# Row norms of a three-layer transformer kernel: column sums and turned scales against matmul means, logarithm and exponential

## The chip, the cores and the metric

One core of one Trainium2 chip runs the whole program. The metric is the device time in microseconds (us), the median over runs.

## The reference, cut to what matters

Three layers are computed on 512 tokens of width 1024. Layer 1 is latent attention with an MLP, layer 2 is window attention with an MLP, and the third (a block of its own) has a wide input projection, attention over compressed, selected and windowed keys, a merge, and a gated feed-forward part. Each stage begins with a norm over the 1024 features of a token:

```python
def rmsnorm(x, g):
    xf = x.astype(jnp.float32)
    y = xf * lax.rsqrt(jnp.mean(xf * xf, axis=-1, keepdims=True) + EPS)
    return (y * g.astype(jnp.float32)).astype(x.dtype)
```

The third layer also normalises its keys and queries over the 64 features of each head (`rmsnorm_2(..., k_norm_g)`, `q_norm_g`), before `rope_2` rotates them.

## The kernel before, in words

Activations lie feature-major: partitions are 128 features, the free axis is the 512 tokens. Weights come as 301 tiles of 128x1024 float32 in the order of use. For each tile ScalarE copies `RAW` to a high part `WH` in fp32r (line 1129), GpSimd subtracts to get a low part `WL` (line 630), and TensorE does three fp32r products for each 128x128 block (`product`, lines 722 to 724): high by high, low by high, high by low. `dense` runs over the outputs of a stage; one output of 8 blocks is 24 matmuls of 512 columns. Outputs go round four PSUM banks (`RING`), so output o+4 waits until VectorE or ScalarE has drained output o. ScalarE keeps three tiles ahead (`AHEAD`): its step for output o can begin when TensorE has finished the tile of output o-1.

A norm's scale is not applied to the input: the raw products are multiplied by it when they are drained. So the scale is needed by the first drain of the stage, some outputs after its start. Before the change it is made thus: ScalarE squares, VectorE adds the squares over the 8 feature blocks (`add_square`, into `ACC` or `TMP`); TensorE sums over partitions into a column for each block of 128 tokens (`sums`, line 765: four fp32 matmuls whose moving operand has one column, each two records in the trace); VectorE adds EPS, ScalarE takes the root (`std`, line 1169), VectorE the reciprocal (`scale_columns`); TensorE turns the broadcast column into a row on all partitions (`scales`, line 778: four fp32 transposes of 128x128); VectorE copies that row to `RBC` (`scale_rows`). The token-major column itself (`RCOL`) is used where values are made token-major.

The head norms of the third layer are the same in small. R32 holds 6 tiles of two heads each. For tile j ScalarE squares, `head_sum(j)` (line 1009) sums per head into columns, three tiles at a time go through `head_var`, `head_std`, `head_scale`, then ScalarE widens the column of scales (`head_widen`, line 1431), and `head_spread(j)` (line 1018) turns it by four transposes. `head_norm`, `head_rotate`, `head_rotated` and `head_split` follow.

The place of each such step in stage `in2` is written by hand: `PE_AFTER`, `ACT_AFTER` and `DVE_AFTER` say after which output an engine does what. Every engine is in order. Other steps there are `compress`: step 1 after output 9 (32 fp32 matmuls), step 2 after output 12, which waits for ScalarE's Silu (`cmp_silu`, in ScalarE's step 11, line 1461), and step 3. Stage `in2` ends with `cmp_scores`, a softmax over compressed keys and the first weight tile of the gates.

Of the kernel before, what the change touches and what calls it, by code (L numbers as in the profile page):

```python
# [32 lines left out]
P = 128  # L33
S = 512
# [244 lines left out]
def program(nc, stream, gains, consts, x, mem, pos_rows, pos_cols, cmp_w1, cmp_w2, out):  # L279
# [4 lines left out]
    with ctx:  # L284
# [11 lines left out]
        WL = tensor(ctx, "WL", [P, RING, TW], F32R)  # L296
        ACC = tensor(ctx, "ACC", [P, S])
# [10 lines left out]
        UNUSED = tensor(ctx, "UNUSED", [P, 1])  # L308
        W2 = tensor(ctx, "W2", [P, HD])
# [53 lines left out]
        with ExitStack() as block2:  # L363
# [5 lines left out]
            with ExitStack() as before:  # L369
# [4 lines left out]
                with ExitStack() as head_scales:  # L374
                    WIDE = tensor(head_scales, "WIDE", [P, 2, S])
                with ExitStack() as q_k_v:
# [12 lines left out]
                    HS = tensor(q_k_v, "HS", [P, NT, NH])  # L389
# [35 lines left out]
        scale_used = signal("scale_used")  # L425

# [109 lines left out]
        def place_turned(name):  # L536

            used, group = {}, 0
            for i, u in enumerate(ATTENTION[name][0]):
# [5 lines left out]
                else:  # L545
# [15 lines left out]
        ACT_AFTER = {2: [("square", 0)], 3: [("square", 1), ("square", 2)], 4: [("square", 3), ("std", 0)],  # L561
                     5: [("square", 4), ("widen", 0), ("widen", 1)], 6: [("square", 5), ("widen", 2)],
                     7: [("rotate", 0), ("std", 1), ("widen", 3)], 8: [("rotate", 1)],
                     9: [("rotate", 2), ("split", 0), ("widen", 4)], 10: [("ya", 0), ("rotate", 3), ("widen", 5)],
                     11: [("cmp_silu", 0), ("split", 1)], 12: [("rotate", 4)], 13: [("ya", 1), ("split", 2)],
                     14: [("rotate", 5)], 15: [("split", 3)], 16: [("ya", 2), ("split", 4), ("cmp_std", 0)],
                     17: [("split", 5)], 19: [("ya", 3), ("cmp_exp", 0)]}
        DVE_AFTER = {4: [("var", 0), ("scale", 0)], 6: [("norm", 0)], 7: [("norm", 1), ("var", 1)],
                     8: [("scale", 1), ("rotated", 0), ("norm", 2)], 9: [("rotated", 1), ("norm", 3)],
                     10: [("split_lo", 0), ("cmp_bias", 0)], 11: [("ya_lo", 0), ("rotated", 2), ("norm", 4)],  # L570
# [3 lines left out]
                     19: [("split_lo", 5), ("cmp_softmax", 0), ("ya_lo", 3)]}  # L574
        IN2_OUTS = list(range(CHANNELS + 12)) + [LAST_V]
# [7 lines left out]
        def squares_sum(norm):  # L583

            return TMP[:, 1, :] if norm == "norm1" else ACC

# [132 lines left out]
        def _(pe):  # L719
# [153 lines left out]
            def mlp(name):  # L873
# [14 lines left out]
                chunk(0, set(), {0: [sums(name)], 1: [scales(name)]})  # L888
# [75 lines left out]
            def late_first(steps):  # L964
# [13 lines left out]
                  after={(1, 2): [sums("in1")], 1: [scales("in1")]})  # L978
# [25 lines left out]
            def head_sum(j):  # L1004
                pe.wait_ge(signal("head_squares"), j + 1)
                squares = (ACC, SQ)[j % 2]
                for b in range(NT):
                    at = b * NH + 2 * j
                    ins = pe.matmul(BANK[6 - j // 3][:, at:at + 2], squares[:, blk(b)], const("head_rows", 0, 2), start=True,  # L1009
                                    stop=True)  # L1010
                ins.then_inc(signal("head_sums"), 1)

            def head_spread(j):
                pe.wait_ge(signal("head_scales_wide"), j + 1)
                if j >= 2:
                    pe.wait_ge(signal("head_normed"), j - 1)
                for b in range(NT):
                    ins = pe.transpose(BANK[6 + j % 2][:, blk(b)], WIDE[:, j % 2, blk(b)], IDENT)
                ins.then_inc(signal("head_spread"), 1)

            def compress(step):
# [18 lines left out]
                else:  # L1040
# [4 lines left out]
            after = {1: [sums("final"), sums("norm1", bank=7)],  # L1045
                     2: [scales("final", column=RMEM), scales("norm1", bank=6)]}
# [19 lines left out]
            pe_steps = {"sum": head_sum, "spread": head_spread, "compress": compress, "cmp_scores": cmp_scores}  # L1066
# [38 lines left out]
            def ffn_part(i):  # L1105
# [4 lines left out]
                  after={0: [sums("norm2")], 1: [scales("norm2")]})  # L1110
# [7 lines left out]
        def _(act):  # L1118
            act.wait_ge(signal("acc_set"), 1)
            act.activation(UNUSED[:], ACC[:, 0:1], ACT.Copy).then_inc(signal("acc_read"), 1)  # L1120

            ahead = [0]
# [37 lines left out]
            def square(norm, m, src, tokens=S, scale=1.0):  # L1160
# [4 lines left out]
                act.activation(squares_of(norm, m)[:, 0:tokens], src, ACT.Square, scale=scale).then_inc(squared, 1)  # L1165

# [58 lines left out]
            def mlp(name, norm_after, gain_after, stage_after):  # L1225
                o0, t0 = plan.out0[name], plan.tile0[name]

                def up(i, keep):
                    for m in range(CH + 1):
                        if m < CH:  # L1230
                            out_of = lambda c: o0 + 16 * c + m
                            keep(m)
                            act.wait_ge(products_done, over(lambda c: plan.out_mark[out_of(c)], i))
# [3 lines left out]
                            if m == 0 and isinstance(i, int) and i == 0:  # L1237
                                std(name)
# [147 lines left out]
            std("in1")  # L1386
            for o in range(6 + EARLY_Q):
                keep_ahead(in1 + o)
                if 1 <= o < 3:
# [21 lines left out]
            std("final")  # L1411
# [991 lines left out]
```

## Time and profile before

| what | value |
|---|---|
| median of 3 runs (lowest, highest) | 1865.19 us (1863.39 to 1865.94) |
| profiled execution, its own time | 1863.88 us |
| its span | 1862.1 us |
| TensorE busy | 1836.1 us, 99% |
| GpSimd busy | 1050.8 us, 56% |
| VectorE busy | 855.2 us, 46% |
| ScalarE busy | 769.0 us, 41% |
| granted TensorE clock | 1.00 |

A matmul's record is longer than what it costs in a row of matmuls, since they are pipelined: what one costs is read from the distance between the starts of neighbours. A row with x8 or x4 is a run of instructions merged into one; its start is that of the first.

### The profile page before, as it was taken

The numbers are of one execution on the slowest core, as the hardware profiler recorded it, in microseconds if no ns is written. First come the engines' busy times: TensorE is split into PE (matmuls) and PEld (weight loads), VectorE is DVE, ScalarE is ACT, GpSimd is POOL, SyncE is SP. The second block draws the span as 40 slices with busy tenths as digits, with TensorE's granted clock in tenths as the row PEclk, the third lists the DMA queues.
The fourth block names the chain that finished last, engine by engine and source line by source line (L and its number), as shares of the span: only waits on it lengthen the run. The fifth ranks groups of instructions, "written<-read, shape, count | busy, mean of one in ns | idle before, by whom it ended". The sixth has DMA issues, their size and how long they took to land.

```text
span 1862.1 us, 26749 instructions
## 1 busy us (share of the span) xinstructions
PE 1836.1 (99%) x9071; PEld 1517.1 (81%) x9071; DVE 855.2 (46%) x1737; ACT 769.0 (41%) x1373; POOL 1050.8 (56%) x1436
## 2 busy tenths in 40 slices
PE   9999999999999999999999999999999999999999
PEld 6876888888888877888888888887788888888887
DVE  7786532222326684322223673787742354444200
ACT  6666542323134674423232453747642342323221
POOL 6862555555546864555555564555565555555553
PEclk9999999999999999999999999999999999999999
DMA  6330233232323212332323222221123223323332
GB/s 226 117 105 1 64 101 102 91 102 90 102 91 101 70 46 70 108 102 91 102 90 101 91 91 91 75 73 35 35 91 102 91 91 101 101 90 94 109 103 78
DMA packets 47582, 168.30 MB, mean 90 GB/s; under 512 B 5632, under 2 KB 5888, under 8 KB 47232
## 3 DMA queue, kind: packets, MB, share of 16 engines
q1 hardware_dynamic: 46512, 164.64, 27.4%
q10 hardware_dynamic: 976, 2.39, 0.5%
q8 instruction: 60, 0.98, 0.2%
q14 instruction: 34, 0.28, 0.0%
HBM read 164.13 MB, written 2.10 MB: 89 GB/s over the span
## 4 chain that ended last, share of the span: by engine, by line
PE 92%; POOL 3%; issue 2%; DVE 2%; ACT 1%; POOLq 0%; ACTq 0%; DVEq 0%
PE bank L722 28%; PE bank L723 27%; PE bank L724 27%; PE bank L814 3%; POOL WL L630 3%; PE bank L854 2%; PE bank L865 2%; PE bank L832 1%; PE bank L827 0%; ACT PROB L1200 0%; PE bank L765 0%; PE bank L1009 0%; DVE PROB L1672 0%; PE bank L1054 0%; PE bank L1026 0%
## 5 line engine op out<-in xcount | busy, mean ns | idle before, releaser
L630 POOL TENSOR_TENSOR WL<-RAW,WH 128x256 fp32r<-128x256 f32 x1208 | 937.2, 808 | 668.6 <-ACT WH L1129 660.7
L722 PE MATMUL bank<-XH,WH 128*128 128x512 f32 x1311 | 520.8, 397 | 1.7 <-DVE KMV L1941 1.5
L724 PE MATMUL bank<-XH,WL 128*128 128x512 f32 x1311 | 510.8, 390 | 0.0
L723 PE MATMUL bank<-XL,WH 128*128 128x512 f32 x1311 | 510.7, 390 | 0.0
L1129 ACT ACTIVATE WH<-RAW 128x1024 fp32r<-128x1024 f32 x301 | 316.0, 1052 | 297.0 <-PE bank L724 293.7
L724 PEld LDWEIGHTS bank<-XH,WL 128*128 128x128 f32 x1311 | 246.1, 188 | 52.1
L722 PEld LDWEIGHTS bank<-XH,WH 128*128 128x128 f32 x1311 | 246.4, 188 | 49.7 <-DVE KMV L1941 1.7
L723 PEld LDWEIGHTS bank<-XL,WH 128*128 128x128 f32 x1311 | 246.6, 188 | 46.3
L722 PE MATMUL bank<-HH,WH 128*128 128x512 f32 x512 | 199.2, 389 | 0.0
L723 PE MATMUL bank<-HL,WH 128*128 128x512 f32 x512 | 199.2, 389 | 0.0
L724 PE MATMUL bank<-HH,WL 128*128 128x512 f32 x512 | 199.2, 389 | 0.0
L1759 DVE TENSOR_TENSOR AB<-TMP 128x512 f32<-128x512 f32 x64 | 45.4, 711 | 241.4 <-ACT TMP L1235 241.2
L1776 DVE TENSOR_TENSOR DT<-bank,RB 128x512 f32<-128x512 f32 x64 | 44.3, 692 | 214.3 <-PE bank L724 214.3
L1235 ACT ACTIVATE TMP<-bank 128x512 f32<-128x512 f32 x64 | 38.2, 597 | 212.7 <-PE bank L724 212.7
L722 PEld LDWEIGHTS bank<-HH,WH 128*128 128x128 f32 x512 | 96.1, 188 | 20.0
L724 PEld LDWEIGHTS bank<-HH,WL 128*128 128x128 f32 x512 | 96.1, 188 | 19.9
L723 PEld LDWEIGHTS bank<-HL,WH 128*128 128x128 f32 x512 | 96.1, 188 | 19.9
L722 PE MATMUL bank<-H2H,WH 128*128 128x512 f32 x176 | 68.5, 389 | 0.0
L723 PE MATMUL bank<-H2L,WH 128*128 128x512 f32 x176 | 68.5, 389 | 0.0
L724 PE MATMUL bank<-H2H,WL 128*128 128x512 f32 x176 | 68.5, 389 | 0.0
L1528 ACT ACTIVATE TMP<-TMP,GV 128x512 f32<-128x512 f32 x22 | 15.9, 724 | 121.1 <-DVE TMP L2030 121.1
L1172 ACT ACTIVATE XH<-X,GV 128x512 fp32r<-128x512 f32 x40 | 28.5, 723 | 71.4 <-DVE X L1714 49.1
(385 smaller groups left out, 2788.0 us busy)
## 6 DMA issues: line engine op xcount, KB each, us to landing
RAW<-stream SPq DMA_DIRECT2D x301, 512.0 KB, 3.4
out<-X SPq DMA_DIRECT2D x8, 256.0 KB, 4.6
X<-x SPq DMA_DIRECT2D x3, 512.0 KB, 8.5
MEM<-mem SPq DMA_DIRECT2D x1, 1024.0 KB, 10.5
W<-cmp_w ACTq DMA_DIRECT2D x1, 1024.0 KB, 4.6
KT<-KR ACTq DMA_DIRECT2D x1, 768.0 KB, 7.6
CT<-consts SPq DMA_DIRECT2D x1, 513.5 KB, 11.0
X<-x SPq DMA_DIRECT2D x2, 256.0 KB, 4.0
```

The costliest lines, as they stand in the source:

```text
L630: ins = pool.tensor_tensor(WL[:, slot, c], RAW[:, slot, c], WH[:, slot, c].bitcast(F32), ALU.subtract)
L722: pe.matmul(dst, lhs[0], rhs[0], start=start, stop=False)
L723: pe.matmul(dst, lhs[0], rhs[1], start=False, stop=False)
L724: return pe.matmul(dst, lhs[1], rhs[0], start=False, stop=stop)
L814: ins = pe.matmul(BANK[SCORES[name][i % ns]][:, u.keys], q, k, start=n_pass == 0, stop=n_pass == len(u.passes) - 1)
L854: ins = pe.transpose(BANK[TURNED_AT[name][j]][:, blk(kb)], row[:, blk(kb)], IDENT)
L865: ins = pe.matmul(BANK[HEAD_OUT[name][pair % 2]][u.out_rows, u.out_cols], u.values[kb], u.turned[:, blk(kb)], start=kb == 0, stop=kb == u. ...
L1129: act.activation(WH[:, slot, :], RAW[:, slot, :], ACT.Copy).then_inc(hi_done, 1)
L1172: act.activation(XH[:, m, :], X[:, m, :], ACT.Copy, scale=gain(norm_gain, m)).then_inc(signal(stage + "_x_hi"), 1)
L1235: act.activation(TMP[:, m % 2, :], BANK[(o0 + m) % RING][:], ACT.Relu).then_inc(signal(name + "_relu"), 1)
L1759: dve.tensor_tensor(AB[:, m % 2, :], TMP[:, m % 2, :], TMP[:, m % 2, :], ALU.mult).then_inc(drained, 1)
L1776: dve.tensor_tensor(DT[:, m % 2, :], BANK[(o0 + 8 + m) % RING][:], RB2[:], ALU.mult).then_inc(drained, 1)
```

## The change: what it does

Six norms (`mlp0`, `in1`, `mlp1`, `final`, `norm1`, `norm2`) get their mean on every row at once. ScalarE copies the added squares to a high part in fp32r (`sum_hi`), VectorE subtracts for a low part (`sum_lo`), and TensorE multiplies both by a 128x128 matrix of 1/1024 (`row_means`: two fp32r matmuls of 512 columns into one bank). ScalarE then takes Ln of bank plus EPS and Exp of minus a half of that, in place in `RBC` or `FINAL` (`row_scale`). Where a token-major column is needed as well (`in1` and `norm1`), TensorE turns `RBC` by four transposes (`turn_row`) and VectorE picks 4 columns (`column_of_row`). `norm1`, whose input is already scaled by `final`, has two multiplications on VectorE ahead of Ln and one behind Exp (`norm1_mean`). The high and low parts lie where `SQ` and `ACC` (or `TMP`) are.

The six tiles of head norms are treated alike: Square, high copy, low part, two matmuls by a block matrix of 1/64 (`head_mean`), Ln and Exp (`head_scale`). `HS`, `head_sum`, `head_var`, `head_std`, `head_widen` and `head_spread` go. `head_norm` reads the scale from SBUF. The four norms of the first layer's start (`in0`, `mem`, `c_kv`, `c_q`) and the norm of the compressed keys stay as they are. At the start VectorE sets `EPSC` and ScalarE writes `MEAN` from `ACC`.

The core of the diff:

```diff
+            def row_means(norm, bank=4):
+                def step():
+                    hi, lo, n = sum_halves(norm)
+                    pe.wait_ge(signal("sum_lo"), n + 1)
+                    weights = MEAN[:, 0:1].to_broadcast([P, P])
+                    pe.matmul(BANK[bank][:], weights, hi, start=True, stop=False)
+                    pe.matmul(BANK[bank][:], weights, lo, start=False, stop=True).then_inc(sums_done, 1)
+                return step
...
+            def turn_row(norm, bank=5):
+                def step():
+                    pe.wait_ge(scale_used, NORM_NO[norm] + 1)
+                    for t in range(NT):
+                        ins = pe.transpose(BANK[bank][:, blk(t)], RBC[:, blk(t)], IDENT)
+                    ins.then_inc(scale_done, 1)
+                return step
...
-                chunk(0, set(), {0: [sums(name)], 1: [scales(name)]})
+                chunk(0, set(), {1: [row_means(name)]})
...
-                  after={(1, 2): [sums("in1")], 1: [scales("in1")]})
+                  after={(1, 2): [row_means("in1")], 2: [turn_row("in1")]})
...
+            def head_mean(j):
+                pe.wait_ge(signal("head_squares_lo"), j + 1)
                 if j >= 2:
+                    pe.wait_ge(signal("head_scales"), j - 1)
+                _, hi, lo = head_squares(j)
+                pe.matmul(BANK[6 + j % 2][:], HEAD_MEAN, hi, start=True, stop=False)
+                pe.matmul(BANK[6 + j % 2][:], HEAD_MEAN, lo, start=False, stop=True).then_inc(signal("head_means"), 1)
...
-            after = {1: [sums("final"), sums("norm1", bank=7)],
-                     2: [scales("final", column=RMEM), scales("norm1", bank=6)]}
+            after = {(1, 2): [row_means("final", bank=5), row_means("norm1", bank=6)], 4: [turn_row("norm1", bank=4)]}
...
-                  after={0: [sums("norm2")], 1: [scales("norm2")]})
+                  after={(1, 2): [row_means("norm2")]})
...
+            def row_scale(norm, dst, bank=4):
...
+                    act.activation(dst, BANK[bank][:], ACT.Ln, bias=EPSC[:]).then_inc(log_done, 1)
+                act.wait_ge(log_done, NORM_NO[norm] + 1)
+                act.activation(dst, dst, ACT.Exp, scale=-0.5).then_inc(scale_used, 1)
...
+                own.then(act.activation(squares, R32[:, j, :], ACT.Square))
+                act.activation(hi, squares, ACT.Copy).then_inc(signal("head_squares"), 1)
+
+            def head_scale(j):
+                act.wait_ge(signal("head_means"), j + 1)
+                if j in (2, 3):
+                    act.wait_ge(signal("head_normed"), j - 1)
+                elif j == 4:
+                    act.wait_ge(signal("head_squares_lo"), 6)
+                own.then(act.activation(HEAD_SCALE[j], BANK[6 + j % 2][:], ACT.Ln, bias=EPSC[:]))
+                act.activation(HEAD_SCALE[j], HEAD_SCALE[j], ACT.Exp, scale=-0.5).then_inc(signal("head_scales"), 1)
...
-        PE_AFTER = {3: [("sum", 0)], 4: [("sum", 1), ("sum", 2)], 5: [("sum", 3)], 6: [("sum", 4), ("spread", 0)],
-                    7: [("sum", 5), ("spread", 1)], 8: [("spread", 2)], 9: [("compress", 1), ("spread", 3)],
-                    11: [("spread", 4)], 12: [("compress", 2), ("spread", 5)], 15: [("compress", 3)],
+        PE_AFTER = {4: [("mean", 0)], 5: [("mean", 1)], 7: [("mean", 2)], 8: [("mean", 3)], 9: [("compress", 1)],
+                    10: [("mean", 4)], 11: [("mean", 5)], 12: [("compress", 2)], 15: [("compress", 3)],
                     18: [("cmp_scores", 0)]}
...
+        ACT_AFTER = {2: [("square", 0)], 3: [("square", 1)], 5: [("square", 2), ("scale", 0)],
+                     6: [("square", 3), ("scale", 1)], 7: [("rotate", 0)], 8: [("scale", 2), ("rotate", 1), ("square", 4)],
+                     9: [("scale", 3), ("rotate", 2), ("split", 0), ("square", 5)], 10: [("ya", 0), ("rotate", 3)],
+                     11: [("scale", 4), ("cmp_silu", 0), ("split", 1)], 12: [("scale", 5), ("rotate", 4)], 13: [("ya", 1), ("split", 2)],
```

In `DVE_AFTER` the six `square_lo` steps (after outputs 2, 3, 5, 6, 8 and 9) take the place of `var` and `scale`; `norm`, `rotated`, `split_lo` and the steps of the compressed keys stay after the same outputs. `prepare_compression` moves from output 3 to output 5.

## Rows read from the trace of the kernel before

**Rows 1.** The page, part 1: busy time, share of span, instructions.

```profile
PE 1836.1 (99%) x9071; PEld 1517.1 (81%) x9071; DVE 855.2 (46%) x1737; ACT 769.0 (41%) x1373; POOL 1050.8 (56%) x1436
```

**Rows 2.** Stretches of `in2`: us, busy PE, PEld, DVE, ACT, POOL, clock, DMA, GB/s.

```profile
1128.00:1200.00 72.00, 72.00 (x375) 60.96 (x374) 37.17 (x59) 38.53 (x57) 34.68 (x44) 1.00 0.25 80
1200.00:1249.00 49.00, 49.00 (x273) 42.50 (x271) 45.88 (x66) 21.42 (x31) 28.17 (x30) 1.00 0.24 79
```

**Rows 3.** Timeline of TensorE at `norm2`: start us, us, line, operands.

```profile
1503.32 0.39 PE L723 MATMUL bank<-XL,WH 128*128 128x512 f32 x1
1503.55 0.39 PE L724 MATMUL bank<-XH,WL 128*128 128x512 f32 x1
1503.78 0.95 PE L765 MATMUL bank<-CT,ACC 128*128 128x1 f32 x8
...
1504.91 0.40 PE L723 MATMUL bank<-XL,WH 128*128 128x512 f32 x1
...
1509.94 0.39 PE L724 MATMUL bank<-XH,WL 128*128 128x512 f32 x1
...
1510.84 0.39 PE L723 MATMUL bank<-XL,WH 128*128 128x512 f32 x1
```

**Rows 4.** Timeline of TensorE at `final` and `norm1`.

```profile
1118.47 0.39 PE L724 MATMUL bank<-XH,WL 128*128 128x512 f32 x1
...
1120.73 0.40 PE L723 MATMUL bank<-XL,WH 128*128 128x512 f32 x1
...
1125.76 0.39 PE L724 MATMUL bank<-XH,WL 128*128 128x512 f32 x1
...
1127.09 0.39 PE L723 MATMUL bank<-XL,WH 128*128 128x512 f32 x1
```

**Rows 5.** Timeline of TensorE at the head sums and spreads.

```profile
1132.10 0.39 PE L724 MATMUL bank<-XH,WL 128*128 128x512 f32 x1
...
1133.46 0.40 PE L723 MATMUL bank<-XL,WH 128*128 128x512 f32 x1
...
1152.17 0.39 PE L724 MATMUL bank<-XH,WL 128*128 128x512 f32 x1
...
1153.92 0.40 PE L723 MATMUL bank<-XL,WH 128*128 128x512 f32 x1
```

**Rows 6.** Timeline of ScalarE: a table load, short and long ACTIVATEs.

```profile
1186.87 1.04 ACT L1129 ACTIVATE WH<-RAW 128x1024 fp32r<-128x1024 f32 x1
1187.93 1.28 ACT L1461 ACT_TABLE_LOAD   x1
1189.23 0.64 ACT L1461 ACTIVATE H<-bank,SM 64x62 f32<-64x62 f32 x2
1189.89 2.57 ACT L1156 ACTIVATE KNH<-R 64x512 fp32r<-64x512 f32 x4
...
1514.35 0.72 ACT L1528 ACTIVATE TMP<-TMP,GV 128x512 f32<-128x512 f32 x1 [7.82 <-DVE TMP L2030]
```

**Rows 7.** Timeline of TensorE: start of output 8, and step 2 of `compress`.

```profile
1160.34 0.48 PE L722 MATMUL bank<-XH,WH 128*128 128x512 f32 x1
...
1192.89 0.32 PE L1035 MATMUL bank<-H,W 64*64 64x62 f32 x2
```

**Rows 8.** Timelines of VectorE, ScalarE and TensorE: waits towards the end of `in2`.

```profile
1199.70 0.69 DVE L2009 TENSOR_TENSOR PROB<-bank,RBC 128x512 f32<-128x512 f32 x1 [1.63 <-PE bank L724]
1201.34 0.63 ACT L1455 ACTIVATE YAH<-PT 128x512 fp32r<-128x512 f32 x1 [4.13 <-DVE PT L2018]
1236.72 0.69 DVE L2009 TENSOR_TENSOR PROB<-bank,RBC 128x512 f32<-128x512 f32 x1 [0.45 <-PE bank L724]
1249.33 0.47 PE L722 MATMUL bank<-XH,WH 128*128 128x512 f32 x1 [0.19 <-POOL WL L630]
```

**Rows 9.** Timelines of ScalarE and VectorE where window attention starts.

```profile
627.64 1.28 ACT L1200 ACT_TABLE_LOAD   x1
628.80 0.08 DVE L1672 DVE_READ_ACCUMULATOR2_ANT SM<- 128x1 f32 x1
```

More of the change, by code:

```diff
@@ L583, in squares_sum, with sum_halves @@
         def squares_sum(norm):
-            return TMP[:, 1, :] if norm == "norm1" else ACC
+            return TMP[:, 1, :] if norm == "norm1" else ACC[:]
+        ROW_NORMS = ["mlp0", "in1", "mlp1", "final", "norm1", "norm2"]
+        def sum_halves(norm):
+            first = 2 if norm == "norm1" else 0
+            hi, lo = (SUMS[:, 2, :], SUMS[:, 3, :]) if first else (SUMS[:, 1, :], SUMS[:, 0, :])
+            return hi, lo, ROW_NORMS.index(norm)
         block = ctx.enter_context(nc.Block())
@@ L1064, in cmp_turn @@
                     ins.then_inc(signal("cmp_turned"), 1)
-            pe_steps = {"sum": head_sum, "spread": head_spread, "compress": compress, "cmp_scores": cmp_scores}
+            pe_steps = {"mean": head_mean, "compress": compress, "cmp_scores": cmp_scores}
             for o, steps in PE_AFTER.items():
@@ L1477, in _ @@
                     keep_ahead(in2 + o)
+                    if o == 1:
+                        row_scale("final", FINAL[:], bank=5)
+                        row_scale("norm1", RBC[:])
                     for what, j in ACT_AFTER.get(o, []):
@@ L1576, in scale_columns, with sum_lo, row_scaled, norm1_mean @@
                     dve.reciprocal(dst[:, 0:nt], STD[:, 0:nt]).then_inc(column_done, 1)
+            def sum_lo(norm):
+                hi, lo, n = sum_halves(norm)
+                dve.wait_ge(signal("sum_hi"), n + 1)
+                dve.tensor_tensor(lo, squares_sum(norm), hi.bitcast(F32), ALU.subtract).then_inc(signal("sum_lo"), 1)
+            def row_scaled(norm):
+                dve.wait_ge(scale_used, NORM_NO[norm] + 1)
+            def norm1_mean(bank=6):
+                row_scaled("final")
+                dve.wait_ge(sums_done, NORM_NO["norm1"] + 1)
+                own.then(dve.tensor_tensor(RBC[:], BANK[bank][:], FINAL[:], ALU.mult))
+                dve.tensor_tensor(RBC[:], RBC[:], FINAL[:], ALU.mult).then_inc(signal("var_done"), 1)
+                row_scaled("norm1")
+                own.then(dve.tensor_tensor(RBC[:], RBC[:], FINAL[:], ALU.mult))
+            def column_of_row(n, bank=5):
+                dve.wait_ge(scale_done, len(NORMS) - len(ROW_NORMS) + n)
+                own.then(dve.tensor_copy(RCOL[:, 0:NT], BANK[bank][:, 0:S:P]))
             def scale_rows(norm, dst, tokens=S, bank=5):
@@ L1803, in _ @@
             in0, memo = plan.out0["in0"], plan.out0["mem"]
+            dve.memset(EPSC[:], EPS)
             dve.memset(ACC[:], 1.0).then_inc(signal("acc_set"), 1)
@@ L1913, in _ @@
             in1 = plan.out0["in1"]
-            scale_columns("in1", D)
-            scale_rows("in1", RBC)
+            sum_lo("in1")
+            row_scaled("in1")
             s1 = SPLIT_AT["in1"]
@@ L2193, in _ @@
             fo = plan.out0["ffn_up"]
+            sum_lo("norm2")
             own.step(dve.memset(GB[:, :, 0:2], 0.0))
```

139 lines of the change are left out of this document (67 added, 72 removed).

## The prediction

> **What bounds the kernel now.** I read the page's busy times first: TensorE is busy for 1836.1 of the 1862.1 us span, ScalarE for 769.0, VectorE for 855.2 and GpSimd for 1050.8 [rows 1]. So time comes out of this kernel where TensorE's queue gets shorter, and goes in where TensorE is made to wait. Then I read the stretches of stage `in2`, where most of the change lies: TensorE is busy for all of 1128 to 1200 us and 1200 to 1249 us. ScalarE has 33.5 us free in the first of them, VectorE 34.8; in the second VectorE has only 3.1 us free [rows 2]. Last I read TensorE's timeline at each place of the old work. The granted clock is 1.00 in both stretches [rows 2].
>
> **What one piece costs.** Dense matmuls start 0.23 us apart (1503.32, 1503.55); over an output the mean is 0.2275, so one output of 24 is 5.45 us [rows 3]. A piece of other work costs what it adds between two dense starts. Without it, L724 and the L723 after next are 0.455 us apart.
> - `sums` for one norm: 1504.91 - 1503.55 = 1.36, less 0.455: 0.905 us [rows 3].
> - `scales` for one norm: 1510.84 - 1509.94 = 0.90, less 0.455: 0.445 us [rows 3].
> - Two `sums` together: 2.26 - 0.455 = 1.805. Two `scales`: 1.33 - 0.455 = 0.875 [rows 4].
> - One `head_sum`: 1.36 - 0.455 = 0.905. One sum with one spread: 1.75 - 0.455 = 1.295, so a spread behind other fp32 work is 0.39; alone I take it at 0.445, as `scales`, since both are four 128x128 transposes [rows 3, 5].
> - New: two fp32r passes of 512 columns are two more dense matmuls, 0.455 us. Their weights are of dense size and type. Nothing of before has a 128x128 weight load in fp32r from one repeated column, so the bounds are 0.455 and 0.905, the last being the whole of the old sum; I take 0.455, since everything else about them is the neighbours'.
>
> **The sum on TensorE.** `mlp0`, `mlp1`, `norm2`: each -0.905 - 0.445 + 0.455 = -0.895, together -2.69. `in1`: the same, and +0.445 for `turn_row`: -0.45. `final` and `norm1`: -1.805 - 0.875 + 0.91 + 0.445 = -1.33. Heads: sum 0 alone 0.905, sums 1 and 2 together 1.805, sum 3 alone 0.905, sums 4 and 5 each with a spread 2 x 1.295, spreads 2 and 4 alone 2 x 0.445, spreads 3 and 5 behind `compress` 2 x 0.39: 7.88 in all, against six pairs at 2.73: -5.15. Total: -2.69 - 0.45 - 1.33 - 5.15 = -9.6 us. All the removed pieces sit between dense matmuls of an engine that doesn't idle there [rows 2 to 5].
>
> **When the scale is ready.** It is wanted by the first drain, and output 4 can't start before output 0 is drained. In `norm2` the first drain had to wait until the turned scale came after output 1, at about 1510.8. Now the means are due a quarter into output 1, some 2 us after 1503.78, ready at about 1506.3. Ln is an ACTIVATE with a bias column, 0.72 us, and Exp is like a plain 128x512 ACTIVATE, 0.63 us [rows 6, 8]. Even with a 1.28 us table load between them RBC is there before 1509.5. In `in1` it is alike; its column `RCOL` waits for a turn after output 2 and is first used when that output is drained. For `norm1` the way is longer: Ln, Exp, two VectorE products of 0.69, Ln, Exp, one more product, with two loads between them some 7.5 us from the means, so 16 us into the stage, while output 4 starts at about 22.7. In the MLPs the scale is first used by the down projection, nine outputs into the stage. All this is hidden under dense outputs; with that cover gone, `norm1` would cost its 7.5 us once. At the kernel's start the `EPSC` memset (4 bytes a partition) and a two-column copy are under the wait for x; I take 0, at most 0.1.
>
> **ScalarE's tables.** This is the dear part of the new work. The trace shows a table load at 1.28 us: the WH copy ahead of it ends at 1187.91, the load starts at 1187.93, and its ACTIVATE at 1189.23 [rows 6]. So a switch costs 1.30. Roots used one load for a norm; now there are 12 pairs of Ln and Exp. No row has Ln, so one load serves both, or every pair has two; bounds for the six heads: 1.3 us or 15.6 us. I take two per pair, the case that can hurt. Then a pair is 0.72 + 0.63 + 2.6 = 3.95 us, six are 23.7, the high copies add 3.8, and the six widenings (0.63 each) go: ScalarE gets some 23.7 us more in a stretch with 33.5 free [rows 2, 6, 8].
> [...]
>
> **Where ScalarE could hold TensorE.** The tightest place is step 2 of `compress`, after output 12: it waits for Silu, which stands behind scale 4 in ScalarE's step 11. From the start of output 8 ScalarE must do: four WH copies 4.2; pairs 2, 3, 4: 11.9; rotates 1 to 3 and split 0, four times four copies of 0.64: 10.3; squares and high copies 4 and 5: 2.5; one YA copy 0.6; Silu's load and its two pieces 1.9. That is 31.4 us. There is 1192.89 - 1160.34 = 32.6, with three spreads (-1.3) and three means (+1.4) in exchange 32.7 [rows 6, 7]. But ScalarE also waits on the way, for VectorE's norms and for the first YA, 1 to 2 us. So TensorE waits 0 to 1.5 us there. I take 0.7. What stands behind that wait is the next dense output, and then all.
> VectorE gets six `square_lo` of 0.69, 4.1 us, all before output 10, where it has most of its 34.8 us free; what goes is small. It must not be late at 1199.70, where it had 1.63 us to spare, since from there to 1236.7 it has hardly a gap, and the chain from output 19 over the softmax, the last Exp, WH and WL ends at TensorE's 1249.33 with no slack [rows 8]. Being late by more than 1.6 us there would cost one for one. `prepare_compression` moved by two outputs runs in free time.
> Window attention: Exp's table is now loaded already in `in1`. The load ended at 628.92, the first row of scores was ready at 628.88, so nothing is won [rows 9].
>
> Sum: -9.6 + 0.7 = -8.9. The profiled execution took 1863.88 (span 1862.1 and 1.8 around it), so about 1855.0 for one like it; it lies 1.3 under the median. For the median: 1865.19 - 8.9 = 1856.3 us.
>
> **Rivals.**
> - *ScalarE or VectorE bind in the head stage.* Speaking for it: the count at `compress` closes within 1.3 us, and VectorE's string behind it has 1.6. If ScalarE's extra waits are 3 to 6 us, TensorE gives back 2 to 6: 1858 to 1862. Against: each wait must be longer than in before.
> - *A table switch costs near double.* If with each load ScalarE stood still for as long again, the 31.4 us at `compress` would gain 7 loads x 1.3 = 9.1, and pair 5, later, 2.6 more; TensorE would wait some 10 to 14: 1865.2 - 9.6 + 13 = 1868.6, slower. It decides from about 1.2 us a load upward (7 x 1.2 + 0.7 is near the gain). Against it: the row has 0.02 us on either side of the load [rows 6]. [...]
> - *The passes are not cheaper.* If a mean costs 0.905, as the old sum, twelve of them return 5.4: 1861.7. If the freed slots were refilled by waits as well, no change: 1865.
> - *More is won.* One load per run of pairs frees ScalarE: no wait at `compress`, -9.6: 1855.6; and if attention's waits shrink a little too, 1853.5.
>
> **How the numbers follow.** Forecast as worked out, 0.62, its own range 1854.5 to 1858; more won 0.13; ScalarE or VectorE bind 0.12; passes not cheaper 0.05; no change 0.03; table switch double 0.05. The predicted time is 1856.3. The range 1853.3 to 1861 takes in the bounds of `compress` (0 to 1.5), the first rival nearly whole, and the 1.3 us between execution and median; about 0.15 is left out. Within 0.2% (3.7 us) a measurement can't tell this kernel from itself. Faster than 1861.5: the first two cases and most of the third and fourth, 0.89; within 0.05; slower 0.06.
>
> **What the profile after would show.** Right: no L765 rows beyond 100 us, pairs of 512-column matmuls 0.23 apart at each place, a dense pitch undisturbed on both sides, TensorE busy about 9.6 us less, table loads of 1.28 before each Ln and each Exp, and a wait for Silu under 1.5 us. Wrong: L722 starts held up in `in2` by a drain or WL, a mean pair that takes 0.9, a VectorE that is late at output 14, or a new TensorE wait at 1240 to 1250.

## The result, and the profile after

The median over 21 runs is 1867.66 us (1865.05 to 1870.1) against 1864.29 us of the kernel before (1863.39 to 1866.09, 21 runs); the ratio is 1.0017, interval [1.0011, 1.0023]. The forecast was 1856.3. That is 3.4 us slower, clear of the noise but small; what is to be explained is 11 us that didn't come. One execution of the last experiment took 6481 us and one of the kernel before beside it 3733, far outside all others; they are in no ratio.

The profiled execution has a span of 1867.1 us, 5.0 more than before. These are the page's busy times (to be read against [rows 1]) and the stretches of stage `in2` (against [rows 2]; columns as there, the clock is the number behind POOL's):

```profile
PE 1835.1 (98%) x8959; PEld 1512.8 (81%) x8959; DVE 865.9 (46%) x1729; ACT 811.1 (43%) x1416; POOL 1059.6 (57%) x1436
```

```profile
1107.00:1128.00 21.00, 18.92 (x75) 14.82 (x74) 13.08 (x16) 16.11 (x21) 12.88 (x16) 0.92 0.32 101
1128.00:1200.00 72.00, 70.21 (x326) 58.16 (x325) 40.57 (x59) 57.76 (x74) 36.09 (x43) 0.98 0.23 74
1200.00:1249.00 49.00, 47.24 (x231) 40.35 (x230) 43.15 (x58) 22.68 (x31) 29.78 (x28) 0.93 0.28 86
```

TensorE now has idle time in all three stretches, and in all three its clock is below 1.00. Its waits, from the view that totals them (total, times, longest), those that are new or longer:

```profile
PE bank L806 <- DVE SUMS L1638: 2.7, 3, 1.7
PE bank L1063 <- ACT H L1514: 1.8, 1, 1.8
PE bank L1081 <- DVE KB L2202: 1.8, 1, 1.8
PE bank L783 <- DVE ACC L1611: 1.3, 1, 1.3
```

L806 is `row_means`; L1063 and L1081 are step 2 of `compress` and `cmp_scores`; L783 is the old `sums`, which the norms of the start keep. And this is TensorE's timeline at the first of these waits:

```profile
1115.41 0.39 PE L742 MATMUL bank<-XH,WL 128*128 128x512 f32 x1
1117.48 0.50 PE L806 MATMUL bank<-SUMS,MEAN 128*128 128x512 f32 x1 [1.67 <-DVE SUMS L1638]
...
1118.62 0.50 PE L806 MATMUL bank<-SUMS,MEAN 128*128 128x512 f32 x1 [0.41 <-DVE SUMS L1638]
...
1119.19 0.48 PE L740 MATMUL bank<-XH,WH 128*128 128x512 f32 x1
1119.47 0.63 PE L741 MATMUL bank<-XL,WH 128*128 128x512 f32 x1
1119.90 0.63 PE L742 MATMUL bank<-XH,WL 128*128 128x512 f32 x1
```

Look at the last two: dense matmuls that start 0.23 us apart elsewhere start 0.43 apart here. The cause is in the windows of 4 us, where the clock is shown; here at this place and at the keys:

```profile
1116.00:1120.00 4.00, 2.12 (x7) 1.40 (x8) 1.91 (x2) 3.97 (x6) 3.85 (x5) 0.92 0.15 60
1120.00:1124.00 4.00, 4.00 (x14) 3.16 (x13) 1.39 (x2) 3.77 (x5) 2.61 (x4) 0.65 0.56 148
1232.00:1236.00 4.00, 4.00 (x22) 4.00 (x20) 3.87 (x5) 0.75 (x1) 4.00 (x5) 0.50 0.34 115
1236.00:1240.00 4.00, 4.00 (x13) 3.20 (x13) 3.87 (x4) 0.00 (x0) 4.00 (x5) 0.65 0.39 108
```

A mean of 0.65 over 4 us is 2.8 us at 0.50 and the rest at 1.00: shorter windows show 0.50 from 1119.5 to 1122.5 and 1.00 from 1123 on. Behind Silu and at the start (the wait at L783) it is:

```profile
1192.00:1196.00 4.00, 2.93 (x13) 2.36 (x14) 3.84 (x6) 3.88 (x8) 0.00 (x0) 0.81 0.42 133
48.00:52.00 4.00, 4.00 (x13) 3.17 (x12) 1.45 (x2) 2.54 (x4) 3.37 (x4) 0.63 0.01 2
```

The other window of each pair has 0.77 (1196 to 1200 us) and 0.95 (44 to 48 us). So behind each of four places of waiting (the two waits of `final` and `norm1` count as one) stands a spell at half clock: 3.4 us three times and 6.8 us behind the keys, 17.0 in all. TensorE is busy throughout these spells (4.00 of 4.00 us in the windows at 48, 1120, 1196, 1232 and 1236 us), so no idle time shows them. In a spell a dense matmul costs 0.427 (2.56 for six, from 1119.90 to 1122.46) in place of 0.2275, so 0.47 of the spell is lost: 8.0 us.

It is not one execution alone. The mean clock of each of the 21 is on record: 0.998 in the one of 1865.05 us, 0.996 in twelve (median 1867.3), 0.995 in six (median 1869.0) and 0.994 in two (1869.2 and 1870.1). Beside e1 the kernel before had 0.997 to 1.000 in 33 executions.

The account of the profiled execution, against the prediction's -9.6 on TensorE: waits of 1.67 + 0.41 for the means of `final` and `norm1`; 0.65 for the mean of `in1` (the rest of L806's 2.7); 1.79 for Silu; 1.75 for the compressed keys; 0.46 more than before at the start; and 8.0 of spells. That is +14.7, so +5.1; measured +5.0. Some small waits of before (0.44 us at 72.18, 0.19 at 1249.33) are gone and not counted, so the account is good to about a microsecond, not to 0.1. The pieces of the -9.6 hold: a mean pair of the heads among its neighbours is two more matmuls at the dense pitch.

```profile
1146.72 0.39 PE L742 MATMUL bank<-XH,WL 128*128 128x512 f32 x1
1146.95 0.39 PE L1046 MATMUL bank<-QN 128*128 128x512 f32 x1
1147.17 0.39 PE L1047 MATMUL bank<-QN 128*128 128x512 f32 x1
```

A second reading gives the same by stages. The copies into `WH` are the same 301 in each kernel, so the start of one copy against the start of the same copy in the kernel before says how far ahead or behind a kernel is there. Beside the changed kernel stands e8, an experiment below, whose mean clock is 1.000 and whose waits in `in2` are nearly gone (the forecasts are the prediction's terms on TensorE, without waits):

| stage | the copy's start before | forecast | changed kernel | e8 |
|---|---|---|---|---|
| `mlp0` | 210.13 to 323.36 | -0.9 | -0.95 | -0.96 |
| `in1`, into window attention | 589.07 to 679.43 | -0.45 | +0.41 | +0.52 |
| `mlp1` | 756.07 to 819.76 | -0.9 | -0.92 | -0.91 |
| `in2` with `final`, `norm1`, heads | 1097.23 to 1300.83 | -6.5 | +5.6 | -6.4 |
| `norm2` | 1457.00 to 1621.91 | -0.9 | -0.93 | -0.93 |

Where nothing waits the forecast is met. The exception is `in1`, which cost time in place of saving some; its mean waits in every version with the new norms, here:

```profile
598.80 0.49 PE L806 MATMUL bank<-SUMS,MEAN 128*128 128x512 f32 x1 [0.65 <-DVE SUMS L1638]
```

**Where each wait comes from.** At `final` and `norm1` the timelines of ScalarE and VectorE:

```profile
1115.26 0.69 DVE L1611 TENSOR_TENSOR TMP<-TMP 128x512 f32<-128x512 f32 x1
1116.65 0.77 DVE L1638 TENSOR_TENSOR SUMS<-ACC,SUMS 128x512 fp32r<-128x512 f32 x1 [0.69 <-ACT SUMS L1199]
1117.34 1.22 DVE L1638 TENSOR_TENSOR SUMS<-TMP,SUMS 128x512 fp32r<-128x512 f32 x1
```

```profile
1115.03 1.04 ACT L1158 ACTIVATE WH<-RAW 128x1024 fp32r<-128x1024 f32 x1
1115.99 0.63 ACT L1199 ACTIVATE SUMS<-ACC 128x512 fp32r<-128x512 f32 x1
1116.53 0.61 ACT L1199 ACTIVATE SUMS<-TMP 128x512 fp32r<-128x512 f32 x1
```

The two sums are complete at 1115.15 (`ACC`) and 1115.95 (`TMP`). TensorE asks at 1115.6, right after its last dense matmul. The first high copy starts at 1115.99, behind a WH copy, then come the second and the two low parts. At `in1` it is the same on a smaller scale: TensorE asks at 598.0, and the low part, started at 597.93, takes 0.81. At Silu, ScalarE's own queue is the reason: two loads for scale 4 and a third for Silu, back to back.

```profile
1186.05 1.06 ACT L1158 ACTIVATE WH<-RAW 128x1024 fp32r<-128x1024 f32 x1
1187.13 1.28 ACT L1482 ACT_TABLE_LOAD   x1
1188.42 0.69 ACT L1482 ACTIVATE ACC<-bank,EPSC 128x512 f32<-128x512 f32 x1
1189.13 1.28 ACT L1483 ACT_TABLE_LOAD   x1
1190.43 0.63 ACT L1483 ACTIVATE ACC<-ACC 128x512 f32<-128x512 f32 x1
1191.08 1.28 ACT L1514 ACT_TABLE_LOAD   x1
1192.37 0.64 ACT L1514 ACTIVATE H<-bank,SM 64x62 f32<-64x62 f32 x2
```

At the keys it is VectorE's string of work from the drain of output 14 to the second copy into `KB`. It had 27.5 us in the kernel before (1199.70 to 1227.23), and TensorE's scores started at 1227.3, as it ended: no wait, but no slack. After, it takes 29.3 (1201.12 to 1230.41), and the wait is 1.75. No operation was added to it: some more of the 512-column operations take 1.1 us and not 0.69. They lie where GpSimd works; the drains that read a bank (`PROB<-bank,RBC`) take 0.69 there too. GpSimd in the kernel before, then after:

```profile
1204.30 3.71 POOL L630 TENSOR_TENSOR WL<-RAW,WH 128x256 fp32r<-128x256 f32 x4 [3.54 <-ACT WH L1129]
1209.46 8.34 POOL L630 TENSOR_TENSOR WL<-RAW,WH 128x256 fp32r<-128x256 f32 x8 [1.46 <-ACT WH L1129]
```

```profile
1204.36 18.14 POOL L648 TENSOR_TENSOR WL<-RAW,WH 128x256 fp32r<-128x256 f32 x16 [4.80 <-ACT WH L1158]
```

After, GpSimd has four tiles in one run through the string, where it had three before (the first row's four pieces, the second's eight; four pieces are a tile). VectorE's second product of rotated 4 falls in a gap of GpSimd before (1208.01 to 1209.46) and into the run after:

```profile
1208.47 0.68 DVE L2064 TENSOR_TENSOR R<-TMP,COS 128x512 f32<-128x512 f32 x1
```

```profile
1209.93 1.23 DVE L2137 TENSOR_TENSOR R<-TMP,COS 128x512 f32<-128x512 f32 x1
```

### The profile page after: what moved, and what is told of

Its sections match the earlier page's. It is cut to its first block, busy times and chain, and to the rows that moved or that the text cites. A ratio compares the mean times of both kernels' runs of the same rounds, so it can differ in the third digit from the quotient of the medians.

```text
span 1867.1 us, 26555 instructions
## 1 busy us (share of the span) xinstructions
PE 1835.1 (98%) x8959; PEld 1512.8 (81%) x8959; DVE 865.9 (46%) x1729; ACT 811.1 (43%) x1416; POOL 1059.6 (57%) x1436
## 4 chain that ended last, share of the span: by engine, by line
PE 89%; DVE 5%; ACT 3%; issue 2%; DMA 0%; SPq 0%; DVEq 0%; ACTq 0%
PE bank L740 27%; PE bank L742 27%; PE bank L741 27%; PE bank L851 3%; PE bank L891 2%; PE bank L902 2%; PE bank L869 1%; DVE ACC L1611 1%; DVE XL L1663 0%; PE bank L864 0%; DMA X<-x 0%; ACT WH L1158 0%; ACT PROB L1244 0%; DVE ML_ L1895 0%; PE bank L1081 0%
```

## The experiments

Theory A: each wait of some 1.8 us is paid twice, as itself and as a spell at half clock. Theory B: the waits cost what they last, and the rest of the loss is elsewhere. Each kernel is the changed one with the edit shown, but for the last. `LATE` stands for the first edit. All times against the kernel before on the same chip.

| run | edit | median us (range, runs) | ratio, interval |
|---|---|---|---|
| e1_late | means of `final`, `norm1` after output 1 | 1863.92 (1861.78 to 1867.02, 11) | 0.9994 [0.9985, 1.0003] |
| e2_silu | Silu ahead of scale 4 | 1865.25 (1862.46 to 1867.09, 11) | 1.0003 [0.9994, 1.0012] |
| e3_both | both | 1861.07 (1860.4 to 1864.08, 11) | 0.9983 [0.9974, 0.9992] |
| e4_fill | spare matmuls in the three waits | 1861.83 (1861.38 to 1863.27, 11) | 0.9984 [0.9975, 0.9993] |
| e5_keys | both, split 2's low parts behind the keys | 1859.6 (1857.56 to 1861.43, 8) | 0.9974 [0.9964, 0.9985] |
| e6_keys2 | and split 1's | 1860.07 (1858.51 to 1861.71, 11) | 0.9976 [0.9967, 0.9985] |
| e7_oldheads | `LATE`, heads as before the change | 1861.2 (1860.3 to 1864.15, 11) | 0.9984 [0.9975, 0.9993] |
| e8_notables | `LATE`, head scales by copies (leaves out the root) | 1855.62 (1855.28 to 1857.49, 5) | 0.9957 [0.9943, 0.997] |
| e9_heads_one | `LATE`, head scales by one function | 1857.41 (1855.93 to 1858.55, 5) | 0.996 [0.9947, 0.9973] |
| e10_all_one | `LATE`, all scales by one function | 1856.36 (1855.82 to 1857.29, 5) | 0.9958 [0.9945, 0.9971] |
| e11_all_one_keys | and split 2's low parts behind the keys | 1857.54 (1856.24 to 1859.33, 5) | 0.9963 [0.995, 0.9976] |
| e12_before_wait | the kernel before, Silu behind rotate 4 | 1870.18 (1869.17 to 1871.68 and one far outside, 7) | 1.0032 [1.002, 1.0044] |

The medians of before were 1864.74 beside the first four, 1864.36 beside the next four and 1864.21 beside the last.

### The first two waits, one by one

```diff
-            after = {(1, 2): [row_means("final", bank=5), row_means("norm1", bank=6)], 4: [turn_row("norm1", bank=4)]}
+            after = {1: [row_means("final", bank=5), row_means("norm1", bank=6)], 4: [turn_row("norm1", bank=4)]}
```

> The changed kernel with one edit: the two pairs of means of final and norm1 stand after the whole of output 1 of in2, not a quarter into it. In the changed kernel TensorE waits there 1.7 and 0.4 us for the low parts of the sums, and the granted clock is 0.5 for 3.4 us behind it. Theory A (each long TensorE wait is paid twice, once as the wait and once more in the half clock that follows it): the wait goes and its half-clock spell too, 2.1 + 1.7 = some 3.8 us less than the changed kernel, about 1864 us, ratio to before 0.9998. Theory B (the half clock has another cause, such as the new form of matmul): only the 2.1 us come back, about 1865.5, and a stretch at 0.5 still follows the means.

```diff
-                     11: [("scale", 4), ("cmp_silu", 0), ("split", 1)], 12: ...
+                     11: [("cmp_silu", 0), ("scale", 4), ("split", 1)], 12: ...
```

> The changed kernel with one edit: in ScalarE's step 11 Silu stands ahead of scale 4. In the changed kernel step 2 of compress waits 1.8 us for Silu, behind scale 4 with its two table loads (3.95 us), and a half-clock spell of 3.4 us follows. Theory A: the wait goes, with it the spell, 1.8 + 1.7 = 3.5 us less, about 1864.2. Whether the later wait for the compressed keys (1.75 us) goes as well is open: it stays if VectorE's own string from output 14 on sets it. Theory B: 1.8 us less, 1865.9, and the spell stays.

> Both edits together. Theory A: 3.8 + 3.5 = 7.3 us less than the changed kernel, about 1860.4, ratio to before 0.998; if the wait for the compressed keys goes too, another 1.8 + 3.4, about 1855. Theory B: about 1863.8.

Against the changed kernel's 1867.7 one edit took 3.7 us, the other 2.4, both 6.6 (the kernel before stood 0.4 higher beside these runs). The first is at theory A's number (3.8) and not at B's (2.1), but the interval of 1.7 us either way doesn't fully part them. The second lies between A's 3.5 and B's 1.8, and doesn't decide; in its profiled execution the Silu wait and its spell are gone, but the keys wait is 2.3 us with a spell of 10 us, not 6.8, behind it. Both together are 0.7 short of A's 7.3 and, by 2.7, past B's 3.9; here the interval parts the two. In e3 the two stretches with those waits are whole again, and the third is as it was:

```profile
1107.00:1128.00 21.00, 21.00 (x94) 17.36 (x93) 12.82 (x16) 16.32 (x20) 12.64 (x15) 1.00 0.32 101
1128.00:1200.00 72.00, 72.00 (x340) 59.92 (x339) 46.97 (x72) 62.04 (x80) 38.15 (x45) 1.00 0.26 81
1200.00:1249.00 49.00, 46.64 (x248) 40.75 (x247) 42.21 (x57) 21.49 (x33) 31.43 (x31) 0.93 0.25 77
```

The waits taken away were 2.1 and 1.8, 3.9 together, and the keys wait grew by 0.6: the rest of the 6.6 is clock. In the profiled execution of e1 the Silu wait stood (1.8 us) and the clock did not fall behind it, and in e2's the waits of `final` and `norm1` (1.68 and 0.42) had no spell either; so a wait of this size doesn't bring a spell each time, and of theory A's "each wait" what holds is that it can be paid twice. That also goes with the wider range of the changed kernel (5.1 us against 2.7).

### The same waits, filled

Seven matmuls of 512 columns into an unused bank go ahead of the means of `final`, eight ahead of step 2 of `compress`, eight ahead of the scores. Nothing else changes, and nobody waits less.

```diff
+                def step():
+                    for _ in range(n):
+                        pe.matmul(BANK[bank][:], MEAN[:, 0:1].to_broadcast([P, P]), XH[:, 0, :], start=True, stop=True)
```

> The changed kernel with its three waits in in2 left where they are, and TensorE kept at work in them: 7, 8 and 8 matmuls of 512 columns (0.23 us each) into a bank that nobody reads stand ahead of the waits for the low parts, for Silu and for the compressed keys. Nothing of the reference's computation is changed. Theory A: the waits cost what they did, filled, so nothing is added beyond 0.3 us, but the three half-clock spells behind them (13.7 us at 0.5) go: 6.8 us less than the changed kernel, about 1861. Theory B: the spells stay, no change, 1867 to 1868.

That is 5.8 us less than the changed kernel, with all the waits' time still spent, and a mean clock of 0.998 to 1.000 in all 11 executions. The filler and what follows, in TensorE's timeline:

```profile
1114.49 1.78 PE L813 MATMUL bank<-XH,MEAN 128*128 128x512 f32 x7
1116.35 0.49 PE L806 MATMUL bank<-SUMS,MEAN 128*128 128x512 f32 x1
...
1118.06 0.39 PE L740 MATMUL bank<-XH,WH 128*128 128x512 f32 x1
1118.29 0.39 PE L741 MATMUL bank<-XL,WH 128*128 128x512 f32 x1
```

The dense matmuls behind it are 0.23 apart. The means start as late after the dense work as without filler; only the clock is different. This run parts the two prices: some 5.6 us of waits stay, some 5.8 of clock go. Theory B has no place for it.

### A wait in the kernel before

```diff
-                     11: [("cmp_silu", 0), ("split", 1)], 12: [("rotate", 4)], 13: ...
+                     11: [("split", 1)], 12: [("rotate", 4), ("cmp_silu", 0)], 13: ...
```

> The kernel before, with one edit: ScalarE does Silu behind rotate 4 in its step 12, not in step 11. Its results are then ready some 3.1 us after TensorE asks for them (two copies ahead of it more, 1.06 and 2.6 us, from 1190.5, with its load of 1.28 and 0.64). Theory A (a wait of some 2 us or more can be followed by a spell at half the granted clock, and costs it again): 3.1 + 1.7 to 3.4, so 1869.2 to 1871 us, with a spell of 3.4 us or longer right behind it. Theory B (the wait alone costs): 1867.5 us and the clock at 1.00. The table's place changes no number of loads.

None of the change is in it. The wait came out at 4.30 us, not 3.1, and behind it the clock fell:

```profile
1198.39 0.37 PE L1035 MATMUL bank<-H,W 64*64 64x62 f32 x2 [4.30 <-ACT H L1461]
```

```profile
1196.00:1200.00 4.00, 1.61 (x10) 1.33 (x11) 2.25 (x3) 3.34 (x5) 1.50 (x3) 0.82 0.49 164
1200.00:1204.00 4.00, 4.00 (x16) 3.25 (x15) 0.00 (x0) 0.00 (x0) 2.28 (x4) 0.76 0.17 44
```

0.18 and 0.24 of 4 us, doubled, are 3.4 us at half clock, worth 1.6: 4.3 + 1.6 = 5.9. By the same two copies into `WH` as above, stage `in2` took 5.7 us more than before. The medians differ by 6.0 (1870.18 - 1864.21), but that nearness is in part luck. This profiled execution has another spell, of 6.8 us at 697 us in the first layers, which cost it 1.6 more, and the two executions with a mean clock of 0.999 took 1869.2 and 1869.3, 5.1 more than before. The interval of the ratio (3.7 to 8.2 us) takes in 4.3 as well as 5.9, so it is the trace, by its clock and the 5.7 us of the stage, that speaks against theory B here, and not the times.

### The keys wait, and what bounds the end of the stage

```diff
-                     15: [("split_lo", 2)], 16: [("rotated", 5), ("cmp_var", 0)],
-                     17: [("ya_lo", 2), ("cmp_keys", 0), ("split_lo", 3), ("split_lo", 4)],
+                     16: [("rotated", 5), ("cmp_var", 0)],
+                     17: [("ya_lo", 2), ("cmp_keys", 0), ("split_lo", 2), ("split_lo", 3), ("split_lo", 4)],
```

> On top of the run with both edits (means of final and norm1 after the whole of output 1, Silu ahead of scale 4), VectorE's low parts of split 2 (two pieces of 1.1 us) go behind the compressed keys. Theory A (each wait of some 2 us is paid twice, once as itself and once more by a spell at half the granted clock behind it): KB is there 2.2 us earlier, the 2.4 us wait ahead of the scores falls under 0.4, the 6.8 us at half clock behind it are gone, and the kernel takes 1861.1 - 2.2 - 3.4 = 1855.5 us (1854.5 to 1857.5), the prediction's number. Rival (the wait alone costs, the clock falls for a reason of its own): 1858.9 and the spell at the scores stays. Rival (the chain over VectorE's low parts and the softmax takes it back at the end of the stage): the scores start earlier, but the end of the stage doesn't, and it stays at 1861.

In the next run `split_lo` 1 is moved from step 14 to step 17 as well.

> As the run before, and the low parts of split 1 (four pieces, 4.7 us together) behind the compressed keys too, ahead of those of split 2. KB then has some 4.5 us to spare. Theory A: the same 1855.5 us as the run before if 2.2 us were enough there, less by what was left of a wait (up to 0.4 and its spell) if not. Rival (the work moved behind the keys delays the last drains and the softmax): TensorE waits at the end of the stage, and it is slower than the run before by 1 to 3 us.

The wait for the keys falls from 2.4 to 1.1 and then to nothing, but another grows at the first weight tile of the gates: 1.9 in e5, and in e6

```profile
1245.95 0.47 PE L740 MATMUL bank<-XH,WH 128*128 128x512 f32 x1 [3.33 <-POOL WL L648]
```

The chain of waits of e6 says why: from 1215.76 on it is all VectorE, to the softmax, then

```profile
1240.20 0.70 DVE KCS L2158
...
1241.47 1.05 ACT WH L1158
1242.59 3.23 POOL WL L648 x4
1245.95 0.47 PE bank L740
```

So the third rival of these expectations held in part: VectorE bounds the stage from output 14 to its end. Moving its work about within the string doesn't shorten it. Of the 5.6 us expected, 1.5 came. The profiled execution of e6 has a spell of 3.4 us behind this new wait; e5's has none behind its waits of 1.1 and 1.9.

### The parts alone

In e7 the functions and the three tables of steps for the heads are those of the kernel before, and `LATE` is in.

> The six row norms new, with the means of final and norm1 after the whole of output 1; the head norms as in the kernel before (column sums, roots, widening, four transposes a tile, and its order of steps). By the prediction's terms the norms give -2.69 - 0.45 - 1.33 = -4.5 us. Theory A: no new wait of 1.8 us is left in the head stage, so all of it is kept: 1864.7 - 4.5 = 1860.2 us (1859.5 to 1861.5). Theory B (the removed pieces are not worth what was read from the distance between starts): the norms give under half of it, 1862.5 or more. If the keys wait, whose slack before was nothing, opens by the 1.3 us that the stage's start is earlier, it is 1861.5 to 1863 with a half-clock spell at the scores.

1861.2, 3.2 less than before, where the prediction's terms give 4.5; the profiled execution has the wait of 0.62 at `in1` and a spell in the first layers that cost it 1.6. VectorE's string is 27.5 us again (1198.06 to 1225.59), there is no keys wait and no Silu wait. So the lengthening of the string belongs to the heads' change. The clock is 1.00 in all of `in2`; the spell in the first layers lies at some 696 to 703 us.

```diff
-                own.then(act.activation(HEAD_SCALE[j], BANK[6 + j % 2][:], ACT.Ln, bias=EPSC[:]))
-                act.activation(HEAD_SCALE[j], HEAD_SCALE[j], ACT.Exp, scale=-0.5).then_inc(signal("head_scales"), 1)
+                own.then(act.activation(HEAD_SCALE[j], BANK[6 + j % 2][:], ACT.Copy))
+                act.activation(HEAD_SCALE[j], HEAD_SCALE[j], ACT.Copy, scale=-0.5).then_inc(signal("head_scales"), 1)
```

> As the changed kernel with the means of final and norm1 after the whole of output 1, but the six head scales are made by two copies in place of Ln and Exp, so that no table is loaded for them: this leaves out the root of the head means, and its output is not the reference's. If the 1.28 us table loads make Silu late, the 1.8 us wait at step 2 of the compression is gone (seven loads are taken away ahead of it), and the time is that of the run with both edits, some 1861 us, the keys wait (2 us, and a half-clock spell) staying as it is: VectorE's string sets it. If ScalarE is late for waits on VectorE and not for its tables, the Silu wait stays over 1 us and it takes 1864 us as the run with the late means alone.

It took 5.4 us less than expected: not only the Silu wait went, but most of the keys wait too (0.25 us left). The expectation had VectorE's string, and with it the keys wait, stay as they were; the string is 27.8 us here. GpSimd's work in the string falls apart into separate pieces again (8.37 us from 1201.69 on), with a gap of 8.65 us ahead of the next:

```profile
1218.71 12.28 POOL L648 TENSOR_TENSOR WL<-RAW,WH 128x256 fp32r<-128x256 f32 x12 [8.65 <-ACT WH L1158]
```

Over all versions with VectorE's order of steps unchanged the keys wait is the string's length less 27.5: 29.3 and 1.75 (changed kernel), 29.3 and 1.78 (e1), 29.9 and 2.31 (e2), 29.9 and 2.36 (e3), 27.8 and 0.25 (e8), 28.2 and 0.63 (e9 and e10), 27.5 and none (before, e7). And the string is the longer the longer GpSimd is busy during it: 13.9 us (before, e7), 16.6 (e8), 17.0 (e9, e10), 18.1 (e1), 18.9 (changed kernel), 20.7 (e2, e3).

### One function for the scale

```diff
-                own.then(act.activation(HEAD_SCALE[j], BANK[6 + j % 2][:], ACT.Ln, bias=EPSC[:]))
-                act.activation(HEAD_SCALE[j], HEAD_SCALE[j], ACT.Exp, scale=-0.5).then_inc(signal("head_scales"), 1)
+                act.activation(HEAD_SCALE[j], BANK[6 + j % 2][:], ACT.Abs_reciprocal_sqrt, bias=EPSC[:]).then_inc(signal("head_scales"), 1)
```

> Late means of final and norm1; the six head scales are made by one function (the reciprocal root, with the EPS bias) in place of Ln and Exp, so the whole reference is computed. A head scale is then one ACTIVATE, and a table stays loaded from one head to the next but for Silu between them: some 3 or 4 loads in place of 12. If the loads are what takes the gain, this repeats the run with copies in their place: no wait at Silu, under 0.4 us at the keys, 1855.6 us (1854.5 to 1857). If it was the order of steps alone, 1864 as with the late means alone.

> As the run before, and the six row norms by the one function too: 6 ACTIVATEs of 0.63 us and 6 or more loads of 1.28 us less on ScalarE, none of it where TensorE was seen to wait. Both theories: no difference to the run before by over 0.5 us (1855.3), the wait at the mean of the first MLP's norm (0.6 to 0.7 us, for VectorE's low part) stays.

> As the run before, and VectorE's low parts of split 2 behind the compressed keys. What is left of the keys wait (0.3 us) goes; if the end of the stage is set by VectorE's string of work, as a wait of 1.9 us for WL at its end said of the same edit with Ln and Exp, nothing comes of it: 1855.3 us, the same within 0.5. If the string is not the bound any more, 1855.0.

The heads' 12 loads become 2 (3 or 4 were expected), and ScalarE has 16.8 us less to do in all (811.1 to 794.3); the whole reference is computed. The times are those of e8 within 2 us, with 0.6 us of keys wait left. e10, the norms done so too, has the lowest median of the kernels that compute the whole reference: 7.9 us less than before, 0.9958 [0.9945, 0.9971]. With five executions each, e9, e10 and e11 can't be told apart. e9 lies 0.4 above its expected range, e10 and e11 1.1 and 2.2 above the expected 1855.3; the profiled executions of e9 and e11 have 10 us of spells outside `in2`, that of e10 3.4. The wait that the expectation of e10 puts at the first MLP's norm stayed, but it is the one of `in1` (0.65 us, at 597.68). The last stretch of `in2` in e10 (the two ahead of it are busy throughout, at 1.00):

```profile
1200.00:1249.00 49.00, 47.93 (x271) 41.69 (x270) 45.14 (x71) 21.48 (x35) 26.13 (x27) 1.00 0.24 76
```

e11 tells the same as e5: the keys wait goes, 1.8 us for WL comes at the end of the stage, nothing is won.

## Why the prediction was wrong, by its own steps

- **The sum on TensorE, -9.6: right in its pieces.** The pairs cost two dense matmuls, and four of the five stages came to their number where nothing waited; `in1` didn't, for the next reason. e10, where the waits are nearly gone, came to 1856.4, and e8 to 1855.6; the rival "the passes are not cheaper" is out. That e10 lands on the forecast of 1856.3 does not make the prediction right: it is another kernel.
- **"When the scale is ready": the step that failed first.** It counted from the means to the scale and never asked whether what the means read was there a quarter into output 1. For `norm2` it was. For `in1`, which the prediction called alike, it was not: 0.65 us of wait. For `final` and `norm1`, the two sums are finished at 1115.15 and 1115.95, and two high copies and two low parts come behind: 2.1 us of wait. The old sums of these two stood after the whole of output 1 [rows 4]. "All this is hidden" had no row behind it for the high copies and low parts ahead of the means.
- **The wait at `compress`: right mechanism, mis-sized.** 0.7 (0 to 1.5) against 1.79. Two loads for a pair were right (24 loads for 12 pairs), and so was a switch at 1.28 to 1.30: an ACTIVATE ends at 1189.11, the load starts at 1189.13 and the next ACTIVATE at 1190.43. Neither rival on the loads came true: double price would be some 2.6 us there, and one load for a run of pairs would show fewer than 24.
- **"It must not be late at 1199.70, where it had 1.63 us to spare": the wrong point.** VectorE was not late there: its idle time ahead of output 14 is 4.93 us after the change, since TensorE is the late one, and 0.39 in e3. The point that mattered is inside the string, at 1227.3, where TensorE asks for the keys the moment they are ready. The prediction read the string's two ends and not its middle. It took the string's length as given too; it grew by 1.8 us without a new operation, and GpSimd's work had closed up behind later WH copies. The rival "ScalarE or VectorE bind" had the right mechanism, and the wrong size, as it charged each wait once.
- **No term for the clock.** [rows 2] show 1.00 and the prediction carried it over to a kernel for which it forecast a wait. The spells cost 8.0 us in the profiled execution, more than all the waits (5.6 in `in2`). Of the 14.7 us between the forecast on TensorE and the measured time this is the greater part. With the waits in `in2` at their true size the sum would have been -9.6 + 5.6 = -4.0; with the loss of the spell behind each as well (1.6 + 1.6 + 3.2) it would have been +2.4, near the +3.4 of the medians.
- **Its own signs.** Three of the signs of being right failed: TensorE is busy 1.0 us less, not 9.6, since the spells lengthen its matmuls; the dense pitch behind the means is not undisturbed; and the wait for Silu is over 1.5. None of the signs of being wrong that it named came: no mean pair took 0.9, VectorE was not late at output 14, and no new wait stood at 1240 to 1250. It had no sign for the clock.
- Right, and of no weight: the MLPs, `norm2`, the start of window attention, and the drains: no dense output was held up by a scale.

What stays open: why a wait of 1.8 us brought a spell at one place or in one execution and not in another (every kernel has a wait of 1.9 us that ends at 695 to 698 us in the first layers; the kernel before and the changed one have their clock at 1.00 behind it, seven of the experiments have a spell there). That long operations of VectorE and GpSimd's work go together is seen in the rows and follows the ScalarE load in e3, e7, e8 and e10, but no run changed GpSimd's work alone, so which of the two holds up the other is not shown.

## What to carry to other kernels

When a step is put earlier for the engine that is the bound, follow its inputs back and not only its result forward: the last addition, each copy behind it and the queue that each stands in. For every wait in a string of work, look up its slack at each place where the bounding engine asks, not at the string's ends. Allow for a new wait of TensorE being paid twice, as the spell behind it came here in some executions and not in others (the wait for Silu, 1.79 us with one in the changed kernel, 1.78 without in e1); where it can't be removed, spare matmuls in it kept the clock here (5.8 us for 23 matmuls), and functions on ScalarE that alternate are to be judged by the loads between them (12 of 1.28 us for the heads here, 2 with the one function).

## What the runs showed of the hardware

- Behind waits of 1.3 to 4.3 us TensorE's granted clock fell to 0.50 for 3.4 or 6.8 us (10 us behind the keys wait in e1 and e2); dense matmuls of 512 columns then start 0.43 us apart, not 0.23. Other waits of the same sizes had no spell. With the three waits of `in2` filled with matmuls the clock stayed at 1.00 in the profiled execution (e4).
- Spells can lie where no edit is: at some 696 to 705 us, starting 1 to 5 us behind a wait of 1.9 us that all kernels have, in e2, e5, e7 and e9 to e12, and not in the others; at about 12 us, behind waits of 1.6 to 2.1, in e2, e9 and e11; at about 48 us, behind one of 1.3, in e6 as in the changed kernel. In e9 the first part of the one at 698 us (ahead of it the clock is 1.00):

```profile
696.00:700.00 4.00, 2.81 (x15) 2.31 (x15) 2.98 (x11) 2.68 (x9) 1.24 (x2) 0.78 0.00 0
```

- In the changed kernel Ln and then Exp is two table loads each time, 1.28 us each (24 for 12 pairs); `Abs_reciprocal_sqrt` with the bias is one ACTIVATE of 0.67 us, and its table stays through Copy and Square (in e9 one load at 1140.03 serves the first five head scales, up to 1182.47; the second comes behind Silu, at 1188.78).
